# Two edits to a two-block transformer kernel: the order of two weight splits around the first layer norm, and the order of score and mask products of masked heads

## The reference

```python
for layer in range(DEPTH):
    shift, scale, gate = ada_modulation(c, ada_w[layer, 0], ada_b[layer, 0])
    h = x * (1.0 + scale) + shift
    y = mixer_ab(h, ...) if layer % 2 == 0 else mixer_c(h, ...)
    x = layer_norm(DN_ALPHA * x + gate * y, ln_g[layer, 0], ln_b[layer, 0])
    shift, scale, gate = ada_modulation(c, ada_w[layer, 1], ada_b[layer, 1])
    h = x * (1.0 + scale) + shift
    y = squared_relu_mlp(h, mlp_w1[layer], mlp_w2[layer])
    x = layer_norm(DN_ALPHA * x + gate * y, ln_g[layer, 1], ln_b[layer, 1])
```

## Time and profile before

| what | value |
|---|---|
| median of 3 runs | 1016.22 us (1016.15 to 1017.5) |
| the profiled execution | 1016.17 us, span 1014.3 us |
| PE busy | 960.2 us, 95% of the span |
| PE weight loads | 779.4 us, 77% |
| DVE busy | 705.2 us, 70% |
| ACT busy | 544.8 us, 54% |
| POOL busy | 58.8 us, 6% |
| PE on the chain that ended last | 72%; DVE 12%, DMA 6%, ACT 6% |
| DMA | 209.09 MB, mean 206 GB/s |

### The profile page before, as it was taken

The page is one execution under the profiler, slowest core; times in us unless marked ns, Lnnn a source line. Parts: engine busy times, 40 slices in busy tenths (PEclk is TensorE's granted clock), DMA queues, the critical chain, the costliest instruction groups (busy, mean ns, idle before and its releaser), DMA issues.

```text
span 1014.3 us, 14630 instructions
## 1 busy us (share of the span) xinstructions
PE 960.2 (95%) x5660; PEld 779.4 (77%) x5660; DVE 705.2 (70%) x1053; ACT 544.8 (54%) x873; POOL 58.8 (6%) x51
## 2 busy tenths in 40 slices
PE   6987997999999999999899999999999999998995
PEld 3663576998898877777798989877888887876784
DVE  3588658876878886667875544588546778797775
ACT  3367744644445354655564546436565666657672
POOL 0001001400000001000332100000000000000000
PEclk9999998999999999999999999999999999999998
DMA  9748676899998589422789965545433345551141
GB/s 350 274 142 312 204 249 194 281 332 315 325 316 319 186 298 299 161 88 84 259 261 268 281 202 194 183 162 190 143 123 127 115 166 194 179 166 63 32 167 41
DMA packets 108212, 209.09 MB, mean 206 GB/s; under 512 B 3728, under 2 KB 37920, under 8 KB 108144
## 3 DMA queue, kind: packets, MB, share of 16 engines
q1 hardware_dynamic: 103808, 193.26, 56.0%
q0 software_dynamic: 4336, 14.90, 5.9%
HBM read 206.96 MB, written 1.18 MB: 205 GB/s over the span
## 4 chain that ended last, share of the span: by engine, by line
PE 72%; DVE 12%; DMA 6%; ACT 6%; issue 3%; SPq 1%; ACTq 0%; DVEq 0%
PE bank L1729 15%; PE bank L1732 14%; PE bank L1735 14%; PE bank L1796 5%; PE bank L1790 4%; PE bank L1793 4%; DVE w_lo L1919 3%; DMA raw<-in_mlp_w 3%; PE bank L1815 2%; DMA raw<-in_ada_w 2%; ACT w_hi L1344 2%; PE bank L1639 2%; PE bank L1837 2%; PE bank L1867 1%; DMA tok<-in_ada_w 1%
## 5 line engine op out<-in xcount | busy, mean ns | idle before, releaser
L1919 DVE TENSOR_TENSOR w_lo<-raw,w_hi 128x2048 fp32r<-128x2048 f32 (+2 forms) x134 | 306.4, 2295 | 156.3 <-ACT w_hi L1344 155.5
L1344 ACT ACTIVATE w_hi<-raw 128x2048 fp32r<-128x2048 f32 (+2 forms) x134 | 248.6, 1858 | 133.3 <-DMA raw<-in_mlp_w 66.1
L1729 PE MATMUL bank<-w_hi,ht_hi 128*128 128x512 f32 (+1 forms) x528 | 146.3, 399 | 2.7 <-ACT full L1408 1.9
L1732 PE MATMUL bank<-w_lo,ht_hi 128*128 128x512 f32 (+1 forms) x544 | 145.8, 391 | 1.0 <-DVE w_lo L1919 0.9
L1735 PE MATMUL bank<-w_hi,ht_lo 128*128 128x512 f32 (+1 forms) x528 | 140.1, 388 | 0.0
L1732 PEld LDWEIGHTS bank<-w_lo,ht_hi 128*128 128x128 f32 x544 | 102.3, 190 | 23.5 <-DVE w_lo L1919 1.8
L1729 PEld LDWEIGHTS bank<-w_hi,ht_hi 128*128 128x128 f32 x528 | 95.1, 190 | 26.2 <-issue 7.7
L1735 PEld LDWEIGHTS bank<-w_hi,ht_lo 128*128 128x128 f32 x528 | 98.8, 189 | 20.6
L1732 PE MATMUL bank<-w_lo,hid_hi 128*128 128x512 f32 x256 | 68.5, 390 | 0.0
L1729 PE MATMUL bank<-w_hi,hid_hi 128*128 128x512 f32 x240 | 64.9, 392 | 0.0
L1735 PE MATMUL bank<-w_hi,hid_lo 128*128 128x512 f32 x240 | 64.2, 390 | 0.0
(11 more groups left out here) (252 smaller groups left out, 1260.4 us busy)
## 6 DMA issues: line engine op xcount, KB each, us to landing
raw<-in_mlp_w SPq DMA_DIRECT2D x64, 1024.0 KB, 6.3
raw<-in_ada_w SPq DMA_DIRECT2D x44, 1024.0 KB, 6.7
raw<-in_a_w_in SPq DMA_DIRECT2D x16, 1024.0 KB, 5.3
raw<-in_c_w_in SPq DMA_DIRECT2D x12, 1024.0 KB, 6.3
raw<-in_b_w_in SPq DMA_DIRECT2D x10, 1024.0 KB, 5.1
raw<-in_ple_w_gate SPq DMA_DIRECT2D x8, 1024.0 KB, 5.0
raw<-in_ab_w_in SPq DMA_DIRECT2D x4, 1024.0 KB, 9.8
tok<-in_ada_w SPq DMA_DIRECT2D x4, 1024.0 KB, 12.8
```

Of the source, the lines that this page charges most:

```text
L1344: nc.scalar.activation(split_parts(n)[0], raw_tile(t), ACT.Copy).then_inc(high_done, 1)
L1729: nc.tensor.matmul(dst, a_hi[:, first + k, rows], hi[:, k, :], start=it["first"] and k == 0, stop=False)
L1732: nc.tensor.matmul(dst, a_hi[:, first + k, rows], lo[:, k, :], start=False, stop=False)
L1919: nc.vector.tensor_tensor(lo, raw_tile(split[n]), hi.bitcast(F32), ALU.subtract).then_inc(low_done, 1)
```

## The change

In the first border only (`s` = 0), three numbers of tiles ahead become smaller, so that DVE and ACT meet the splits of A and B later. In the scores step, all score products of a masked pair are issued first and then all its mask products; the score product of the second token half now has `start` off, and the wait for the sparse mask stands between the two groups.

```diff
     def last_tiles(s):
 
-        y[0](1, 3, ts=(0,))
+        y[0](1, 3 if s else 1, ts=(0,))
         if s == 0:
             columns(1, 1, (7,))
-        y[1](1, 2, ts=(0,), spare=True)
+        y[1](1, 2 if s else 0, ts=(0,), spare=True)
         norm_ln(s, 0)
         y[0](1, 2, ts=(1,))
         y[1](1, 1, ts=(1,))
...
     ada_tiles(2)
-    y[1](0, 3, ts=(1,))
+    y[1](0, 2, ts=(1,))
     last_tiles(0)
...
-                    if mode == "sparse":
-                        pe.wait_ge(mask_ready, 1)
+                    masked = mode in ("causal", "window", "sparse")
                     for t in range(T):
                         m = head_cols(mode, t)
-                        masks = {"causal": [(t * P, maskb[:, 2, :])],
-                                 "window": [(0, maskb[:, 2 - t:3, :].rearrange("p a n -> p (a n)"))],
-                                 "sparse": [(0, smask[:, t, 0:m])]}.get(mode, [])
                         done = []
                         for j in range(2):
...
                             done.append(nc.tensor.matmul(bank[b][:, t * S:t * S + m], qkt[part, qc, t * P:(t + 1) * P],
-                                                         qkt[part, kc, 0:m], start=True, stop=not masks))
-                        for j in range(2):
-                            b, _ = it["banks"][j]
-                            for o, mask in masks:
-                                done[j] = nc.tensor.matmul(bank[b][:, t * S + o:t * S + m], maskb[:, 0, :], mask, start=False, stop=True)
+                                                         qkt[part, kc, 0:m], start=t == 0 or not masked, stop=not masked))
+                    if mode == "sparse":
+                        pe.wait_ge(mask_ready, 1)
+                    if masked:
+                        for t in range(T):
+                            m = head_cols(mode, t)
+                            o, mask = {"causal": (t * P, maskb[:, 2, :]),
+                                       "window": (0, maskb[:, 2 - t:3, :].rearrange("p a n -> p (a n)")),
+                                       "sparse": (0, smask[:, t, 0:m])}[mode]
+                            for j in range(2):
+                                b, _ = it["banks"][j]
+                                done[j] = nc.tensor.matmul(bank[b][:, t * S + o:t * S + m], maskb[:, 0, :], mask, start=False, stop=t == T - 1)
```

## The result

| | median | runs | ratio to before, with its 95% interval |
|---|---|---|---|
| before | 1016.68 us | 20 | |
| changed | 1010.50 us | 20 | 0.9939 [0.9928, 0.9951] |

The change makes the kernel 6.2 us faster (0.0061 x 1016.7), with an interval of 5.0 to 7.3 us. The forecast was 6.0. The profiled execution of the changed kernel took 1012.22 us (span 1010.4), so it lies 1.7 above its median; set against the profiled execution of before it shows only 4.0 of the 6.2.

The account below looks back on a forecast made before the run. PE, busy 95% of the span, was taken as the bound, with a hole at the first border from DVE's order. Border 3.0 plus masks 3.0 made 6.0: 1016.2 - 6.0 = 1010.2 us, range 1007.6 to 1013.3.

Parts of the forecast that it names:

- The hole and the first transposes: First border: DVE evicts from 149.15, `u` is ready at 153.86, 5.8 earlier; first transposes start at 154.6 without idle time.
- The second transposes and B: First border: second transposes at 164.6, 3.9 earlier; second MLP tile's low part at 166.8 after 0.8 wait; gain 3.0.
- One idle stretch of 2.2: First border: PE's product of the first MLP tile ends near 162.4, then PE idles 2.2 until the second transposes.
- The masks: Masked heads: 0.3 saved per pair (scores 0.20, masks 0.09), 10 of 16 pairs on the path, together 3.0.
- rival 1: First border: PE's new idle time brings back the low clock, costing 1.5, so 1011.7; chance 0.24.
- Rival 2: Masked heads: the new order gives nothing, as overhead belongs to each product; 1013.2; chance 0.08.
- rival 3: First MLP: weights come at their own rate, so PE waits there for the border's gain; 1013.2; chance 0.08.
- Rival 5: First border: slower, to 1021, if the low clock holds over 12 us behind the second transposes; chance 0.02.
- Rival 6: First border: an overlooked DVE wait on PE or ACT holds the norm; at best the masks' 3.0 remains.

Follow-up runs that it names:

- after: The changed kernel's first profile against the kernel before; median 1010.50 us, ratio 0.9939, profiled execution 1012.22 us.
- after_again: The changed kernel run again unaltered as a yardstick, with a second profile; 1010.73 us, 0.9946 of the kernel before.
- after_third: The changed kernel run again unaltered as a yardstick, with a third profile; 1011.46 us, 0.9950 of the kernel before.
- border_only: The kernel before with only the three new numbers of tiles ahead at the first border, masks as before; 1014.05 us, 0.9968.
- before_again: The kernel before run again unaltered, for a second profile; 1016.16 us.
- before_third: The kernel before run again unaltered, for a third profile; 1018.58 us.
- after_fourth: The changed kernel run again unaltered as a yardstick, with a fourth profile; 1010.23 us, 0.9931 of the kernel before.
- masks_only: The changed kernel with the three numbers of tiles ahead as before, so only the new score and mask order; 1013.91 us, 0.9978 of the kernel before.
- both_borders: The changed kernel with the border's edit at the second layer's border too; 1012.92 us, 0.9968 of the kernel before.
- score_split: The changed kernel with the 256-column score products of masked heads cut in two of 128; 1011.24 us, 0.9943 of the kernel before.

## Why the prediction was right, point by point

**The hole and the first transposes: right.** DVE waits 0.74 for PE's bank ahead of the eviction; `u` comes ahead of PE, the first transposes start without a wait and at the clock of 1.00. `u` ends at 154.65 where I had said near 153.3, but the value product behind the third sparse pair is later too: from there the forecast was 153.86 - 119.07 = 34.79, and `after` has 154.65 - 120.02 = 34.63. In `after_again` the projection's last tile came 1.4 later against the value product than in `after_third`; DVE had no wait there, and PE started the transposes 0.26 late.

**The second transposes and B: right to 0.1.** Forecast were 10.0 from the first transposes to the second ones (164.6 - 154.6) and 12.2 to B's group. `after_third`, at full clock, has 164.65 - 154.63 = 10.02 and 12.25; the wait ahead of B's group was to be 0.8 and is 0.69. From the end of the projection's products to B's group the kernel before takes 169.88 - 154.57 = 15.31 (its products end where the idle stretch begins), so the gain is 15.31 - 12.25 = 3.06; forecast 3.0, `border_only` 3.3 with an interval of 1.7 to 4.8.

**One idle stretch of 2.2: wrong in shape.** I let PE run A's products up to 162.4 and wait once. It waits 0.56 for the ada tile, whose end I had near 158.0, then 0.76 for the low rows, where I had no wait, and then 1.78. The end is the same, since DVE sets it.

**The masks: right.** A window pair saves 0.31, with the forecast at 0.20 for scores and 0.09 for masks (measured 0.21 and 0.10). The causal stage is 187.52 long in the mean of the profiles without the new masks (before, before_again, before_third, border_only) and 185.08 in `after`, `after_again`, `after_third` and `after_fourth`: 2.4 for 8 pairs, as forecast. That the third sparse pair's saving is lost behind DVE, and that of the first two at the tile ahead of it, came as said in the profile of `after`, not in every execution (see below). `masks_only` measures 2.2 (interval 0.9 to 3.6) where I had 3.0.

**The rivals.** The clock (rival 1) falls at the new border in two of the four profiles of the changed kernel, at 165.3 in `after` and at 163.3 in `after_fourth`, and of the three other kernels with the same order there in `both_borders` and `score_split`, not in `border_only`. The three without it (`border_only`, `after_again`, `after_third`) have the same length from the second transposes to the MLP, 10.5; `after`, `after_fourth` and `both_borders`, with a low stretch of some 3.4, have 11.0 to 11.1, and `score_split` has 12.25. Its low stretch is twice as long (columns as in the earlier trace rows, the granted clock is 0.50):

```profile
163.30:169.90 6.60, 5.88 (x28) 5.91 (x29) 5.86 (x9) 2.13 (x5) 1.04 (x2) 0.50 0.58 187
```

So the low clock costs 0.6 at this border in three profiles and 1.8 in one; I had priced it at 1.5, out of a low stretch of up to 5.5. These are the prices less what the wait for B hides (0.7, forecast 0.8). The 56.13 of `after_again` has another source: 0.3 ahead of the first transposes and 0.3 ahead of the second ones, behind the late tile. The rival's mechanism is there, then, in part of the executions, and its price was of the right size. The forecast of 1010.2 and the rival's 1011.7 are too near each other for the time to tell, and that the median lies at the forecast is in part luck. Rival 2 fell by `masks_only` and by the pair's rows, rival 3 by the profiles of before, whose MLP is as long. Rival 5 would need a low stretch of over 12 us; the longest in the first border of any profile is the 6.8 of `before` and `masks_only`, with the old order, and with the new one the 6.6 of `score_split`. Rival 6 is excluded by the rows.

**The sum.** 3.06 for the border, 2.4 for the causal pairs, 0.3 for the fourth sparse pair (from the value product to the first transposes are 35.33 in `border_only` and 35.06 in `after_third`) and 0.3 for the first window pair make 6.1; measured 6.2 [5.0, 7.3]. This is the sum at full clock, and the last term is the pair's own saving, of which no profile shows that it arrives. By the means of the table, with the low clock in two of the four profiles, the border gives 3.0 with the fourth sparse pair in it and the causal stage 2.4, so 5.4 are seen in stages.

What stays open is how much of the window and early sparse pairs' saving arrives. From the group at 79.12 before to the value product at 119.07 are 39.5 to 40.0 us in four profiles with the old masks and 38.4 to 40.8 in ten with the new ones, as the ada tile near 114 us lands earlier or later. The mean gain of 0.3 is far inside that.

## What to carry to other kernels

Follow a hole in PE back to the engine ahead of it and ask which of its instructions nobody needs yet; moving these behind the urgent one wins the hole, but they come back as a wait later, so the gain is the hole less what comes back: 5.3 - 2.3 here, and at the second border 0.9 - 2.8, a loss by the same edit. Once an engine works without a break between two points, only its sum of work counts, and its order inside no longer does; while it still has a wait between them, work moved into that wait can be free. Group short products by kind, and judge a stage by its own distance in several profiles, since a stretch that waits for weights now and then can vary by more than the change is worth.

## What of the hardware was not expected

- POOL's subtraction of two 128x2048 tiles (4.60 us) held a DVE instruction of 128x8 elements for 3.38 us. The nominal 2.3 us of relief for DVE became a loss on the path.
- Which idle places bring the low clock changes between executions of the same program. The profiles of the changed kernel have it near 35.6, 100.5, 165.3 and 673.9 us in one, near 101.0 alone in the next, near 64.4, 101.9, 163.3 and 921.1 in another. Behind nearly the same idle times at the border (0.5 to 0.7, 0.8 and 1.8 us) it came in four profiles of six, and lasted some 3.4 us in three of them and 6.6 in one.
- A group of 64-row fp32 score products costs 0.2 us more where 128-row products follow it, bf16 or fp32, than where its like does, and the way back costs 0.1 us; the four groups of a pair had two changes from 64 to 128 rows and two back, and one of each was saved.
